# Two-block transformer on one core: the relative bias written and read through GpSimd's queue, and sliding attention whose scores, maxima and exponentials run one more unit ahead

## The reference, cut to what matters

```
def gmlp_chunk_mixer(u_raw, v_raw, v_norm_g, w_s, b_s):
    u = jax.nn.gelu(u_raw)
    v = layer_norm(jax.nn.gelu(v_raw), v_norm_g)
    ...
    sv = jnp.einsum("gts,bcsgd->bctgd", ws, v) + b_s...        # 8 groups, chunks of 128 tokens
    return u * sv.reshape(B, S, GM_WIDTH)

def swa_sink_attention(q, k, v, sinks, rel_bias):              # 8 heads, 2 KV heads, window 128
    ...
    scores = jnp.einsum("bnqkgd,bnskd->bnkgqs", q, kb) * (HEAD_DIM ** -0.5)
    bias = rel_bias.astype(jnp.float32)[bucket]                # by distance query - key
    scores = scores + bias[None, None]
    scores = jnp.where(valid[None, :, None, None], scores, MASK_VALUE)
    m = jnp.maximum(jnp.max(scores, axis=-1, keepdims=True), sink)
    p = jnp.exp(scores - m)
    denom = jnp.sum(p, axis=-1, keepdims=True) + jnp.exp(sink - m)
    probs = (p / denom).astype(vb.dtype)
    return jnp.einsum("bnkgqs,bnskd->bnqkgd", probs, vb)...

def second_block(x, ...):
    proj = rms_norm(h, attn_norm_g) @ w_in                     # 512 tokens, 1024 -> 3840 columns
    u_raw, v_raw, q, k, v, gate_a, gate_b = jnp.split(proj, SPLIT_POINTS, axis=-1)
    a = gmlp_chunk_mixer(...)
    b = swa_sink_attention(q, k, v, attn_sinks, rel_bias)
    merged = sigmoid(gate_a) * (a @ w_proj_a) + sigmoid(gate_b) * (b @ w_proj_b)
    h = h + merged @ w_out
    h = h + hierarchical_moe(...)                              # 16 experts
    return rms_norm(h, final_norm_g)
```

## Time and profile before

| | |
|---|---|
| time, median of 3 runs | 3449.92 us (3447.57 to 3478.59) |
| the profiled execution | 3460.93 us, its span 3459.0 us |
| PE busy | 3153.3 us, 91% of the span |
| VectorE busy | 2018.1 us, 58% |
| ScalarE busy | 1115.6 us, 32% |
| GpSimd busy | 209.1 us, 6% |
| TensorE clock granted, mean | 0.91 of full speed |

### The profile page before, as it was taken

How to read it: one execution, slowest core, us unless ns; L and a number is a source line. 1 busy time by engine, 2 the same in 40 slices (tenths; PEclk the granted TensorE clock), 3 DMA queues, 4 the chain that set the end, 5 groups by cost and what they waited for, 6 DMA issues and landing times. The chain is left out here.

```text
span 3459.0 us, 37239 instructions
## 1 busy us (share of the span) xinstructions
PE 3153.3 (91%) x13388; PEld 2366.3 (68%) x13388; DVE 2018.1 (58%) x2636; ACT 1115.6 (32%) x1638; POOL 209.1 (6%) x66
## 2 busy tenths in 40 slices
PE   6999899998899998999899998999996787969885
PEld 4888686555488886888686555488875555747774
DVE  5777713553277777777613553377774533557776
ACT  3222222434222123222221435221213323336665
POOL 0000000000000000000000000000000000016663
PEclk8999999766999999999998768999998878989998
DMA  5232122000132222222222000232314201249995
GB/s 152 85 109 97 44 69 60 25 1 1 49 110 97 85 97 86 97 85 97 57 68 49 25 1 1 73 110 85 109 37 97 77 25 49 73 168 333 324 331 209
DMA packets 235202, 324.16 MB, mean 94 GB/s; under 512 B 56256, under 2 KB 203720, under 8 KB 222664
## 3 DMA queue, kind: packets, MB, share of 16 engines
q1 hardware_dynamic: 229896, 312.12, 28.0%
q0 software_dynamic: 4608, 8.40, 0.7%
q10 hardware_dynamic: 576, 2.10, 0.2%
HBM read 316.82 MB, written 14.16 MB: 96 GB/s over the span
## 5 line engine op out<-in xcount | busy, mean ns | idle before, releaser
L1939 DVE SCALAR_TENSOR_TENSOR x_T<-acc,x_T 128x512 f32<-128x512 f32 x352 | 242.9, 691 | 206.1 <-PE acc L909 205.9
L878 PE MATMUL score<-h_hi,gate_hi 128*128 128x512 f32 x704 | 278.6, 396 | 34.2 <-DVE h_lo L1893 29.2
L1919 DVE RECIPROCAL recip_tile<-exp_tile 128x512 f32<-128x512 f32 x88 | 295.1, 3353 | 6.5
L879 PE MATMUL score<-h_lo,gate_hi 128*128 128x512 f32 x704 | 277.4, 394 | 0.0
L880 PE MATMUL score<-h_hi,gate_lo 128*128 128x512 f32 x704 | 277.0, 393 | 0.0
L878 PE MATMUL score<-h_hi,up_hi 128*128 128x512 f32 x704 | 274.0, 389 | 0.2 <-DVE up_lo L1876 0.2
L879 PE MATMUL score<-h_lo,up_hi 128*128 128x512 f32 x704 | 273.9, 389 | 0.0
L880 PE MATMUL score<-h_hi,up_lo 128*128 128x512 f32 x704 | 273.9, 389 | 0.0
L907 PE MATMUL acc<-hid_hi,down_hi 128*128 128x512 f32 x640 | 251.6, 393 | 8.8 <-DVE x_T L1939 8.8
L909 PE MATMUL acc<-hid_hi,down_lo 128*128 128x512 f32 x640 | 251.6, 393 | 0.0
L908 PE MATMUL acc<-hid_lo,down_hi 128*128 128x512 f32 x640 | 251.1, 392 | 0.0
(11 more groups left out here) (375 smaller groups left out, 6636.5 us busy)
## 6 DMA issues: line engine op xcount, KB each, us to landing
weights<-in_ffn_w_gate SPq DMA_DIRECT2D x44, 1024.0 KB, 5.3
weights<-in_ffn_w_up SPq DMA_DIRECT2D x44, 1024.0 KB, 5.4
weights<-in_ffn_w_down SPq DMA_DIRECT2D x44, 1024.0 KB, 5.5
arena<-in_expert_w_gate SPq DMA_DIRECT2D x32, 1024.0 KB, 5.9
arena<-in_expert_w_up SPq DMA_DIRECT2D x32, 1024.0 KB, 6.2
weights<-in_expert_w_down SPq DMA_DIRECT2D x30, 1024.0 KB, 5.7
weights<-in_w_in SPq DMA_DIRECT2D x23, 1024.0 KB, 5.3
weights<-in_w_out SPq DMA_DIRECT2D x12, 1024.0 KB, 5.2
```

The source lines that it names most:

```text
L878: mm(ps, hi[:, kc, cols], h_hi[:, kc, :], start=kc == 0, stop=False, skip_group_check=True)
L879: mm(ps, hi[:, kc, cols], h_lo[:, kc, :], start=False, stop=False, skip_group_check=True)
L1919: V.reciprocal(rt[:, :], et[:, c, :])
L1939: V.scalar_tensor_tensor(x_T[:, c, :], acc[c % 2][:, :], 0.5, x_T[:, c, :], ALU.mult, ALU.add).then_inc(acc_free[c % 2], 1)
```

## The change

Three edits, all in the second block.

1. The two bias DMAs and the waits before and between them go from SP's program (behind load 3) to the start of GpSimd's program.
2. PE issues `scores` of three units before step 0 and of unit n+3 in step n. ScalarE does `exps` of two units first and of unit n+2 in step n. VectorE does `maxima` of units 0 and 1 and `normalize` of unit 0 first, and `maxima` of unit n+2 and `normalize` of unit n+1 in step n. The waits on the buffers are unchanged.
3. VectorE's half of `split_second` for loads 9 to 15 goes from the end of steps 3, 7, ... 27 to the end of steps 4, 8, ... 28; load 16's stays behind the last step. ScalarE's half stays where it was.

```
-                if n == 3:
-                    sp.wait_ge(relrow_ready, 1)
-                    sp.dma_start(rel_dram, rrow.unsqueeze(1).broadcast_to([8, P, 384])).then_inc(rel_stored, 16)
-                    sp.wait_ge(rel_stored, 16)
-                    sp.dma_start(bias_t, bass.AP(rel_dram.tensor, 127, [[383, P], [384 * P, 8], [1, 256]])
-                                 ).then_inc(bias_loaded, 16)
...
         def _(pool):
             pool.sem_inc(ids_free, 1)
+            pool.wait_ge(relrow_ready, 1)
+            pool.dma_start(rel_dram, rrow.unsqueeze(1).broadcast_to([8, P, 384])).then_inc(rel_stored, 16)
+            pool.wait_ge(rel_stored, 16)
+            pool.dma_start(bias_t, bass.AP(rel_dram.tensor, 127, [[383, P], [384 * P, 8], [1, 256]])
+                           ).then_inc(bias_loaded, 16)
...
                 scores(0)
                 scores(1)
+                scores(2)
                 for n in range(NSW):
-                    if n + 2 < NSW:
-                        scores(n + 2)
+                    if n + 3 < NSW:
+                        scores(n + 3)
                     turns(n)
...
                 exps(0)
+                exps(1)
                 for n in range(NSW):
-                    if n + 1 < NSW:
-                        exps(n + 1)
+                    if n + 2 < NSW:
+                        exps(n + 2)
...
                 maxima(0)
+                maxima(1)
+                normalize(0)
                 for n in range(NSW):
+                    if n + 2 < NSW:
+                        maxima(n + 2)
                     if n + 1 < NSW:
-                        maxima(n + 1)
-                    normalize(n)
+                        normalize(n + 1)
...
-                    if n % 4 == 3:
-                        split_second(7 + n // 4 + 2)
+                    if n % 4 == 0 and n >= 4:
+                        split_second(7 + n // 4 + 1)
+                split_second(7 + NSW // 4 + 1)
```

## The result

The changed kernel takes 3427.39 us, the median of 4 runs (3398.52 to 3429.36). The kernel before, on the same chip, took 3463.78 us, the median of 4 runs (3447.57 to 3478.59). The ratio is 0.9856, with a 95% interval of 0.9811 to 0.9902. Ratios leave out executions over 1.5% above the fastest of their kernel, which the medians include. The change is a gain of about 1.4%, not the 2% that I forecast, and the time lies above my range.

What follows compares the result with a forecast made beforehand. PE, busy 91% of the span, was held up before the q tickets by late loads and in sliding attention by VectorE's normalize. Gains 15 + 37.7 + 11.2 + 3 = 66.9 us from 3449.9 gave 3383.0 us, range 3366 to 3410.

Steps and rivals of the forecast that it cites:

- SP's freedom: Before the first q matmul: with the bias DMAs off SP, loads 4 and 5 go out earlier, gaining 15 us.
- Transfers therefore overlap rather than take turns strictly: On the DMA engines: the bias write runs beside loads 3, 4 and 5, supporting 15 us rather than 10.6.
- the loads gain nothing: Rival, chance 0.10: the write slows the q loads; time 3398 us, or 3394 with a gain of 10.6.
- the 10.6: Gain in us before the first q matmul if write and load packets take turns and load 4 lands at about 2673.
- The bias in time: At VectorE's first maximum: the bias by GpSimd arrives with 17 to 44 us of cover, at no cost.
- GpSimd's 16 us for 1024 pieces: GpSimd's own work for each bias DMA, write and read back, bounded at 16 us if not hidden.
- The sliding attention: Second block: seven holes removed, 37.7 us; six slow steps made fast, 11.2; spatial tickets starting at full clock, 3.
- The slack of 3.0 us: Sliding attention, behind a load's low part: VectorE's normalize ends 3.0 us before PE wants it.
- Everything behind 2955 us follows PE: After the second block's changed part: all the rest moves up as a whole, with no further gain or loss.
- the 66.9: Whole kernel: the forecast gain in us, 15 + 37.7 + 11.2 + 3.
- the first term: The 15 us gain before the first q matmul from taking the bias DMAs off SP.
- ten us more on either side: Range of the whole time: allowance added to 3377 to 3397 us for one median of few runs.

Runs made afterwards that it cites:

- the small write: Changed kernel with the mask row stored once (12 KB), read back as overlapping copies: 3401.17 us, ratio 0.9812 to the kernel before; repeated, 3394.36 us, 0.9801.
- the write head by head: Changed kernel with the bias write issued as eight DMAs of one head each, without a wait between them: 3455.29 us in one execution.

## Why the prediction was wrong

**SP's freedom, forecast 15, measured -1.9.** This is the step that failed. From the mask row to the first q matmul it was 2695.09 - 2633.74 = 61.35 us, and is 2714.36 - 2651.12 = 63.24. The sentence at fault is "Transfers therefore overlap rather than take turns strictly", read from 236 and 285 GB/s. Both windows show loads with all of their bytes issued ahead of the write or after its end. No row showed a load issued during the write, the very case that the change makes. What the runs show in its place: only the half of load 3 that lies on the other eight engines overlaps with the write. The half on the write's engines gets nothing for 14.5 us and then one packet of 0.05 us for each of 0.71, so it landed after 34.5 us instead of 6.6. With a write of 12 KB the first q matmul comes 17.6 us sooner, so the write alone took the term away. The rival "the loads gain nothing", to which I gave 0.10, is what happened; but the 10.6 that I worked out for packets taking turns let load 4 alone be late. I had looked past load 3: before the change it was issued ahead of the write by its place on SP, so the old order protected it. On another queue the write goes out the moment the mask row is ready, 2.5 us ahead of load 3. The changed order was to be had from the text of the two programs; the price was not.

**The bias in time, forecast at no cost: right.** It was issued at 2687.51 and landed 6.5 us later, far ahead of the first maximum at 2759.13 (VectorE's timeline). GpSimd's 16 us for 1024 pieces didn't show: the issues took 1.30 and 0.96 us, the first with VectorE busy for 1.85 of the 2 us from 2652 on (the windows). The Trainium skill ("SBUF — State Buffer", section "SBUF: two separate sides") has GpSimd blocked while VectorE runs an instruction in a two-port mode. No such block is seen in this trace; whether any of VectorE's instructions there ran in that mode, no row shows.

**The sliding attention, forecast 37.7 + 11.2 + 3 = 51.9, measured 55.5** (258.2 us less 202.65, from the first q matmul to ScalarE's copy of load 16). The wait of 38.4 us is gone. The 32 groups of twelve wide matmuls take 92.1 instead of 104.7 us, 12.6 less for 11.2. The spatial tickets run from 2814.65 to 2833.4 instead of 2817.75 to 2838.7, some 2 us less for 3. The remaining 2.5 us are short waits and narrow matmuls. The slack of 3.0 us that I gave VectorE held: no step behind a load waits.

**"Everything behind 2955 us follows PE": off by 4.6 us.** From ScalarE's copy of load 16 to the end it was 505.7 us and is 510.3. The rest behind the stretch was 414.3 and 413.8 in the two kernels with the old sliding attention, and 416.2 to 418.9 in the eleven others. Most of it lies in the experts (380.3 us before, 384.3 after, from the first gather to the end), where DMA moves over 300 GB/s and PE's wait for `mine_lo` grows from 33.3 to 36.0 us. I have no cause for it, and no run was made for it.

**The base.** Of the 35.3 us by which the profiled executions missed the 66.9, 16.9 are the first term, 4.6 the end, -3.6 the sliding attention and 17.4 the first block. I had given "ten us more on either side" for one median of few runs. The start of the stretch lies between 2570.9 and 2625.5 us in thirteen executions, so that allowance was too small by half or more: by the stretch and the rest, the changed kernel lies 50 us under before, while the medians of two sets of runs say 36 and 53. The base moved too: the kernel before had a median of 3449.92 us over three runs and 3463.78 over four. With the first base, 3449.9 - 50 = 3400 would have lain inside my range, so that the time lies above it is in part the base's doing. The first term is wrong on either base.

## What to carry to other kernels

A DMA that is slow by its shape, not by its bytes, can hold up a load issued after it on another queue nearly until its own end: first nothing of the load was served on its engines, then one short packet for each long one. Look at the order of issue, at the long transfer's share and rate, and at the packets of both queues. Then make the transfer small (store once, let the read overlap), or put it behind the loads that are wanted soon. Before moving a DMA to a freer queue, ask which loads its old place put ahead of it. Where a kernel's time wanders, compare a stretch between two marks around the change, not whole executions.

## What was not expected of the hardware

**The same code takes a different time from one execution to the next, by its granted clock.** Two executions, the changed kernel and the second of the small write, are alike up to 1960 us (PE busy 112.57 and 112.61 us, clock 0.82 from 1840 us on). Then, in the attention of layer 2, one is granted 0.54 and the other 0.79. The same windows of both:

```profile
1840.00:1960.00 120.00, 112.57 (x490) 68.46 (x488) 72.45 (x193) 41.76 (x123) 0.00 (x0) 0.82 0.13 36
1960.00:2120.00 160.00, 159.77 (x494) 90.64 (x493) 71.54 (x245) 53.77 (x191) 0.00 (x0) 0.54 0.00 1
```

```profile
1840.00:1960.00 120.00, 112.61 (x489) 68.65 (x488) 72.10 (x192) 41.87 (x123) 0.00 (x0) 0.82 0.13 36
1960.00:2120.00 160.00, 149.87 (x613) 87.69 (x612) 79.69 (x268) 81.46 (x229) 0.00 (x0) 0.79 0.00 1
```

In the same 160 us one did 494 matmuls and the other 613. A mean of 0.54 is the low level (0.50, 1.2 GHz) with a little of the high one (1.00, 2.4 GHz). PE was busy for 159.77 of the 160 us there, and over each 20 us the granted clock was 0.50 to 0.59; in the other execution it was 0.53 to 1.00. What decides this no run shows. The w_out loads of that layer took 299.8, 316.9, 320.3 or 341.1 us over the thirteen executions, a few levels and nothing between.

**The turns of two queues are counted in packets, and one packet can take some fifteen times as long as another.** The write by GpSimd had packets of 4.6 KB and 0.71 us, the same write by ScalarE of 1.5 KB and 0.22 us, load 3 of 1 KB and 0.05 us. The engines gave each queue as many packets as the other, but only 14.5 us after the load's issue.

**A write of 1.5 MB from eight partitions takes 35 us and half of the DMA engines.** The share of 0.50 agrees with the Trainium skill ("DMA: Bandwidth & Descriptors", section "Why a DMA increments its semaphore by 16 and not by 1"), by which a transfer whose slowest dimension is 8 runs on eight engines. With a slowest dimension of 128 (the write head by head) the share rose to 1.0, as the page has it, but the transfer got slower, 59 us, which the advice to use all sixteen (same page, section "Rules for kernel authors") wouldn't lead one to expect.

**SP's issuing can be held up by a transfer that isn't its own.** To hand out the first three of the q DMAs (256 KB each) SP took 1.97 us with the small write, 23.40 us with the write under way, and 47.12 us with the write head by head. (All eight took 14.91, 31.63 and 55.42 us, but the fifth also waits for a v ticket of PE.)
